# An mLSTM stage on one core: VectorE takes the output residual a step later, and four other steps change place

## What is computed

```
proj = modulate(rms_norm(x)) @ w_in          # attention q,k,v; mLSTM q,k (conv + silu), v, o gate, gates
y_attn = axial_gqa_attention(q_a, k_a, v_a)  # 8 heads, softmax over 512 keys
h_fw, h_bw = mlstm(q, k, v, i, f), the same on the reversed sequence   # 4 heads of 128
h = rms_norm_per_head(h_fw + h_bw) * norm_g * sigmoid(o_m)
mix = concat([y_attn, h]) @ w_out            # 512 + 512 rows of w_out
x = x + g1 * mix
x = x + g2 * ffn(modulate(rms_norm(x)))      # follows, not touched
```

## Time and profile before

| | us |
|---|---|
| median of three runs | 1611.53 |
| the profiled execution's own time | 1612.63 |
| its span, first to last instruction | 1610.8 |
| PE busy in the span | 1534.1 (95%) |
| DVE busy | 1026.3 (64%) |
| ACT busy | 654.8 (41%) |
| mean granted TensorE clock | 0.978 |

### The profile page before, as it was taken

One profiled execution on the slowest core, in us unless ns is written; L12 is line 12 of the kernel. 1 busy time (PEld: TensorE's weight loads), 2 busy tenths in 40 slices (PEclk: granted clock), 3 DMA queues, 4 the chain that ended last, 5 costly groups with the idle time before them and its releaser, 6 DMA issues. The chain is left out here.

```text
span 1610.8 us, 25858 instructions
## 1 busy us (share of the span) xinstructions
PE 1534.1 (95%) x10752; PEld 1363.9 (85%) x10752; DVE 1026.3 (64%) x1436; ACT 654.8 (41%) x1051; POOL 24.6 (2%) x22
## 2 busy tenths in 40 slices
PE   7999999998998999999999899999878999999997
PEld 7998778878998999999888777767666999999876
DVE  5533345775446787777665666675567888885454
ACT  5423443333324222222343455545544555554343
POOL 0000000000000000000000011000000000000000
PEclk9999998999998999999999899999999999999999
DMA  4321004342330333232444213110102233332332
GB/s 175 103 82 53 14 23 149 125 161 82 105 105 31 109 126 129 99 131 73 138 150 155 82 47 105 53 34 27 40 26 82 90 105 106 106 105 79 92 92 79
DMA packets 37699, 147.61 MB, mean 92 GB/s; under 512 B 4304, under 2 KB 4432, under 8 KB 27856
## 3 DMA queue, kind: packets, MB, share of 16 engines
q1 hardware_dynamic: 37440, 144.92, 27.1%
q0 software_dynamic: 144, 1.05, 0.2%
HBM read 143.86 MB, written 2.10 MB: 91 GB/s over the span
## 5 line engine op out<-in xcount | busy, mean ns | idle before, releaser
L565 PE MATMUL ps<-t 128*128 128x258 f32 (+4 forms) x2160 | 692.5, 321 | 32.1 <-DVE t L2248 8.3
L567 PE MATMUL ps<-t 128*128 128x258 f32 (+4 forms) x2160 | 681.9, 316 | 0.0
L566 PE MATMUL ps<-t 128*128 128x258 f32 (+4 forms) x2160 | 681.7, 316 | 0.0
L565 PEld LDWEIGHTS ps<-t 128*128 128x128 f32 (+1 forms) x2160 | 411.8, 191 | 75.4 <-issue 31.5
L567 PEld LDWEIGHTS ps<-t 128*128 128x128 f32 (+1 forms) x2160 | 411.3, 190 | 27.1
L566 PEld LDWEIGHTS ps<-t 128*128 128x128 f32 (+1 forms) x2160 | 412.3, 191 | 24.6
L2200 DVE TENSOR_TENSOR t<-t 128x1024 fp32r<-128x1024 f32 (+2 forms) x122 | 208.0, 1705 | 240.3 <-ACT t L1501 240.3
L1501 ACT ACTIVATE t<-t 128x1024 fp32r<-128x1024 f32 (+2 forms) x122 | 175.9, 1441 | 187.6 <-PE ps L567 175.3
L1451 PE MATMUL ps<-t 128*128 128x256 f32 x504 | 142.7, 283 | 0.0
L1449 PE MATMUL ps<-t 128*128 128x256 f32 x504 | 142.5, 283 | 0.1
L1450 PE MATMUL ps<-t 128*128 128x256 f32 x504 | 141.3, 280 | 0.0
(11 more groups left out here) (321 smaller groups left out, 1840.7 us busy)
## 6 DMA issues: line engine op xcount, KB each, us to landing
t<-in_W SPq DMA_DIRECT2D x75, 1024.0 KB, 4.9
t<-in_W SPq DMA_DIRECT2D x62, 512.0 KB, 3.6
t<-in_W SPq DMA_DIRECT2D x100, 256.0 KB, 3.7
t<-in_W SPq DMA_DIRECT2D x4, 644.0 KB, 3.9
t<-in_XT SPq DMA_DIRECT2D x8, 264.0 KB, 6.1
out<-t SPq DMA_DIRECT2D x8, 256.0 KB, 2.9
t<-in_ROPE POOLq DMA_DIRECT2D x1, 1024.0 KB, 5.3
t<-in_CONS SPq DMA_DIRECT2D x1, 423.0 KB, 9.2
```

The lines of the kernel that those rows point to most:

```text
L565: pe.matmul(out, wh, xh, start=first, stop=False)
L566: pe.matmul(out, wh, xl, start=False, stop=False)
L567: return pe.matmul(out, wl, xh, start=False, stop=last)
```

## The change

Six edits in the lists of PE, ACT and DVE (nothing is computed in another way):

1. PE: `head_turn(3)` comes before `w2b_part(3, range(3))` instead of after it.
2. ACT, attention step 13: the split of v5,3 comes before `gqa_exp(14)` instead of after it.
3. ACT, end of step 15: a load of the exponential's function table is written there; in the program before, that load stands before the first `weigh`.
4. ACT, step 16: the last v evacuation comes before the four `prep` copies and the split of wo2a,0 instead of after them.
5. The split of wo2b,1 comes in step 30 (ACT) and 31 (DVE) instead of 32.
6. DVE: the residual (with its split) comes in steps u % 4 == 2 instead of 1, the low part of a finished head in phase 7 instead of 6, and the loop has one step more.

```diff
@@ PE @@
                     if u == 35:
                         pe.wait_ge(S["tl_h"], 16)
+                        head_turn(3)
                     w2b_part(u - 32, range(3))
                 if u >= 12 and u % 8 == 4:
                     head_turn(u // 8 - 1)
-            head_turn(3)
@@ ACT, attention @@
                 if u >= 1:
                     beside_attention(u - 1)
+                if u == 13:
+                    split(gq_split(u))
                 if u < 15:
                     gqa_exp(u + 1)
-                if gq_split(u) is not None:
+                if gq_split(u) is not None and u != 13:
                     split(gq_split(u))
...
                     prep(0, 0)
                     prep(0, 1)
+                    ac.preload_act_table_set(EXPLN)
                 if u == 16:
+                    beside_attention(16)
                     for piece in range(2, 6):
                         prep(0, piece)
                     split(AT["wo2a", 0])
-            beside_attention(16)
@@ ACT, mLSTM @@
-                if u == 32:
+                if u == 30:
                     split(AT["wo2b", 1])
                 if u >= 8 and u % 8 in (0, 1, 6):
                     tail(u // 8 - 1, u % 8)
@@ DVE @@
-                if phase == 6:
+                if phase == 7:
                     dv.wait_ge(S["y_hi"], hd + 1)
...
-            for u in range(39):
+            for u in range(40):
...
-                    if u % 4 == 1:
+                    if u % 4 == 2:
                         next(side)
-                if u == 32:
+                if u == 31:
                     split(AT["wo2b", 1])
...
-                if u >= 8 and u % 8 in (1, 3, 5, 6):
+                if u >= 8 and u % 8 in (1, 3, 5, 7):
                     tail(u // 8 - 1, u % 8)
```

## The result

The changed kernel took 1592.26 us (median of four runs, 1589.57 to 1597.10) against 1611.42 (four runs, 1610.37 to 1613.09): ratio 0.9883, 95% interval 0.9854 to 0.9913, so 1.2% faster. The forecast was 1594.4. The profiled execution took 1589.84 (span 1588.1). A later set of five runs of the same kernel gave 1594.01 (1591.45 to 1597.35), ratio 0.9899, interval 0.9882 to 0.9917.

A forecast was written before the change was run, and what follows sets the result against it. The loop was taken as bound by waits between PE and DVE, no engine full. Terms 4.9 + 1.6 + 3.5 + 4.2 + 1.9 + 1.0 = 17.1 us, from 1611.53 to 1594.4; 80% range 1591 to 1602.

The forecast's parts named there:

- The start: Attention step 13 to the loop's first sums: PE's 2.64 us stall goes, first sums come 4.9 us earlier (bounds 2.6 to 6.2).
- Eight units: Three loop stretches of eight units: weighing ahead of DVE's wait cuts PE's idle time; gains 1.6, 3.5 and 4.2 us.
- The late split before unit 28: Last eight units of the loop: DVE's split (1.23 us) is uncovered there, leaving PE about 2.3 us idle.
- The end: From the last tile to k = 3 of w2b: k = 3 starts at 11.4 instead of 13.32 us, gaining 1.9.
- So the division starts at 3.0, 1.2 earlier: Behind the last tile: with ACT's and DVE's splits done sooner, the last division starts 3.0 us after it, not 4.2.
- The clock behind k = 3: Twelve matmuls run at clock 0.65 because of 2.3 us idle before; full clock makes 3.9 of 4.93 us, gaining 1.0.
- The clock did not stay low: Rival, chance 0.20: the granted clock stays low in the stretches at 0.86 and 0.83; gain only 11.5 us, 1600.0.
- DVE was the bound: Rival, chance 0.10: DVE bounds the whole loop, half of the loop's 9.3 us goes; gain 12.4, 1599.1 us.
- the main case: Chance 0.64: all terms hold, 1594.4 us, own range 1591 to 1598; DVE becomes the bound in the last eight units.
- The slower case: Chance 0.03: residual and split stand uncovered between weighings PE needs, all eight places; 13 us slower, 1625; needs 2.5 idle per tile.
- The table was not loaded twice: Rival of nothing much, chance 0.03: preloaded table loaded a second time, ACT's queue takes back the start; about 1609 us.
- The table load's drain: Before the loop: the skill's drain of about 1380 ns would put ACT 1.4 us later, the start's gain an estimated 3.9.

The follow-up runs named there:

- edit 6 alone: The kernel before with only DVE's residual in the step behind PE's tile and the low part in phase 7; median 1600.18 us, ratio 0.9922.

## Why the prediction was right or wrong

The forecast of a gain of 17.1 us met 17.6 in the stretches that the change touches, and 19.2 and 16.4 between medians. That it is so close is in part luck: the last eight units gave 0.85 more than forecast, and the first units took 0.4 back. Step by step:

- **The start, 4.9 forecast, 4.83 measured.** Right, with its split too: 4.29 for the stall and the clock behind it, 0.27 for the table load, 0.27 for the evacuation. The stretch of the earlier trace rows at 0.87 is at 1.00 now. What I left out is that the loop's first units can get longer: they kept their low clock and are 0.4 to 0.6 us longer in all kernels with 3.48 us or more of idle time before the first sums. They are 1.2 us shorter than before, at clock 1.00, where 1.49 us are left (14.92 against 16.13).
- **Eight units, 1.6, 3.5 and 4.2 forecast; 1.73, 3.70 and 5.05 measured.** Right in mechanism and nearly in size. The late split before unit 28 is the gap that I placed there (2.3 forecast, 2.12 measured). My 15.5 for the last stretch was 0.85 too long; no run splits that miss further.
- **The end, 1.9 forecast, 1.84 measured, but for the wrong reason.** The step that failed is "So the division starts at 3.0, 1.2 earlier", which I gave to edit 5. The place at 3.0 was right (2.8). But the division is 1.8 earlier through edit 6, which takes the gate and the last weighing from behind the tile, and edit 5 puts it 0.43 later again. In the end as a whole: 13.75 less 1.53 (edit 6), less 0.74 (edit 1 beside it), plus 0.43 (edit 5) is 11.91. I had seen that the high part is queued behind ACT's split (1.7 in my count) and did not ask what the order without edit 5 would give once the gate had moved.
- **The clock behind k = 3, 1.0 forecast, 0.87 measured.** Right in size: at full clock DVE's next split sets the pace. The reason that I gave for the low clock, the 2.3 us of idle time before, does not hold by itself: edit 6 alone has them and full clock.
- **The rivals.** The clock did not stay low in the last eight units in any kernel with edit 6, and was 0.83 there in all four profiles without it; so that rival fell. (The first units, at 0.84, are the part of it that came true; the forecast had put no gain there.) DVE was the bound in the last eight units alone, as in the main case. The slower case needed 2.5 us of idle time per tile; there were 0.5 to 3.3 per two tiles. The table was not loaded twice.
- **The table load's drain.** The page of the Trainium skill (ScalarE: Activation LUTs, What ACT_TABLE_LOAD costs) would have made the start an estimated 1.0 us longer. The trace does not show this drain: the next instruction, a copy, starts 1.30 us after the load's start (1117.69 to 1118.99), and in the kernel without edit 3 the exponential itself does (1125.69 to 1126.99). The start is as forecast without the drain.

## What to carry to other kernels

Where an engine waits for another's long piece of work, put behind that wait only what nobody is waiting for: here one step of delay for a result that is needed four steps later was worth 10 us, because weighings that PE needed next had stood behind it. Read the gain of an idle gap together with the clock behind it: behind 3.48 us of idle time the first eight matmuls of the loop took 2.09 us, behind 1.49 us they took 1.16. And when several edits touch one queue, cost each against the order that the others leave, not against the old one: edit 5, costed against the old order, looked like part of a gain of 1.2 us, and in the new one it costs 0.43 (in the old order it was not run by itself).

## What was not expected of the hardware

The same instructions ahead of the change reached step 13 between 1093.72 and 1100.66 us in thirteen profiles, while the start and the end behind it repeat to a few hundredths and the loop within 0.2; the mean granted clock of the span goes with the total (0.985 at 1588.1 us and 0.981 at 1593.7 for the changed kernel). The clock records ahead of step 13 say more: they have 34 us at 1.2 GHz in the earliest profile (1093.72), 38 to 41 in the four at 1095.16 to 1096.90 and 44 to 48 in the eight from 1098.78 on. So most of the difference goes with the clock there, but not all: the six profiles with 48 us still lie 1.5 us apart. Why the clock differs was not tested. Idle time alone doesn't say where the clock falls: PE stood 2.33 us before k = 3 in edit 6 alone and ran at full clock behind it, and stood 2.32 us in the kernel before and ran at 0.65.
